# Recurrent gates as three products of rounded and residual parts in place of native fp32, with the first half of the convolution one weight chunk earlier

## What is computed

```python
xc = causal_depthwise_conv(x_lru, conv_w, conv_b)       # 4 taps, 1024 channels
xb = xc.reshape(B, S, 8, 128)                           # 8 blocks of 128 channels
r = sigmoid(einsum('bsgi,gij->bsgj', xb, w_a) + b_a)    # 8 products 128x128 by 128x256
i = sigmoid(einsum('bsgi,gij->bsgj', xb, w_x) + b_x)    # 8 more
log_a = -8 * r * softplus(-lam)
a = exp(log_a)
u = sqrt(-expm1(2 * log_a)) * (i * xc)
h_t = a_t * h_(t-1) + u_t
```

## Time and profile before

| what | value |
|---|---|
| median of 3 runs | 1424.68 us (1423.48 to 1426.31) |
| profiled execution | 1427.16 us |
| its span, first to last instruction | 1425.4 us |
| TensorE busy in the span | 1418.2 us (99%) |
| VectorE, ScalarE busy | 854.3 us (60%), 718.3 us (50%) |
| mean granted TensorE clock | 0.998 of full |

### The profile page before, as it was taken

One profiled execution on the slowest core, in us unless ns is written; L12 is line 12 of the kernel. 1 busy time (PEld: TensorE's weight loads), 2 busy tenths in 40 slices (PEclk: granted clock), 3 DMA queues, 4 the chain that ended last, 5 costly groups with the idle time before them and its releaser, 6 DMA issues. The chain is left out here.

```text
span 1425.4 us, 17665 instructions
## 1 busy us (share of the span) xinstructions
PE 1418.2 (99%) x7194; PEld 1249.3 (88%) x7194; DVE 854.3 (60%) x897; ACT 718.3 (50%) x858; POOL 24.8 (2%) x44
## 2 busy tenths in 40 slices
PE   9999999999999999999999999999999999999999
PEld 7888888888899888998899988998888888888887
DVE  5555545656566655655555655565667787565654
ACT  6644544545545444444344544454664674665642
POOL 2000000000000000000000000000000001000000
PEclk9999999999999999999999999999999999999999
DMA  9455465657556666666666666665555556545574
GB/s 353 157 171 164 152 207 187 194 187 254 192 200 199 205 201 201 203 199 203 205 195 206 205 201 202 203 203 197 195 191 183 171 190 201 183 149 175 184 233 132
DMA packets 78016, 279.16 MB, mean 196 GB/s; under 512 B 8704, under 2 KB 9728, under 8 KB 77552
## 3 DMA queue, kind: packets, MB, share of 16 engines
q1 hardware_dynamic: 76000, 273.06, 57.9%
q0 software_dynamic: 784, 3.08, 0.6%
q10 hardware_dynamic: 1152, 1.90, 0.4%
HBM read 275.91 MB, written 2.10 MB: 195 GB/s over the span
## 5 line engine op out<-in xcount | busy, mean ns | idle before, releaser
L1031 DVE TENSOR_TENSOR w_lo<-raw,w_hi 128x1024 fp32r<-128x1024 f32 x508 | 620.0, 1224 | 520.2 <-ACT w_hi L733 516.3
L733 ACT ACTIVATE w_hi<-raw 128x1024 fp32r<-128x1024 f32 x508 | 534.7, 1056 | 641.2 <-PE banks L420 449.1
L418 PE MATMUL banks<-w_hi,xa 128*128 128x512 f32 x752 | 291.8, 388 | 0.5 <-DVE w_lo L1031 0.5
L418 PE MATMUL banks<-w_hi,xb 128*128 128x512 f32 x768 | 291.8, 380 | 0.0
L419 PE MATMUL banks<-w_lo,xb 128*128 128x512 f32 x768 | 291.1, 379 | 0.0
L420 PE MATMUL banks<-w_hi,xb 128*128 128x512 f32 x768 | 291.1, 379 | 0.0
L420 PE MATMUL banks<-w_hi,xa 128*128 128x512 f32 x752 | 286.0, 380 | 0.0
L419 PE MATMUL banks<-w_lo,xa 128*128 128x512 f32 x752 | 286.0, 380 | 0.0
L442 PE MATMUL banks<-xa,w_hi 128*128 128x512 f32 x1024 | 242.3, 379 | 0.0
L442 PEld LDWEIGHTS banks<-xa,w_hi 128*128 128x128 f32 x1024 | 184.3, 190 | 20.8
L420 PEld LDWEIGHTS banks<-w_hi,xb 128*128 128x128 f32 x768 | 145.2, 189 | 20.6
(11 more groups left out here) (195 smaller groups left out, 605.5 us busy)
## 6 DMA issues: line engine op xcount, KB each, us to landing
raw<-in_weights SPq DMA_DIRECT2D x511, 512.0 KB, 3.9
h<-in_x SPq DMA_DIRECT2D x2, 1024.0 KB, 10.4
arena<-in_x_turned SPq DMA_DIRECT2D x7, 256.0 KB, 6.5
result<-stage ACTq DMA_DIRECT2D x6, 256.0 KB, 4.8
arena<-in_final_norm POOLq DMA_DIRECT2D x1, 1024.0 KB, 7.1
raw<-in_weights SPq DMA_DIRECT2D x2, 256.0 KB, 4.5
arena<-in_gla_b_gate POOLq DMA_DIRECT2D x1, 512.0 KB, 8.3
arena<-in_lru_w_a POOLq DMA_DIRECT2D x1, 512.0 KB, 9.6
```

The source lines that it names most:

```text
L418: pe.matmul(o, xh[:, kt, xs], woven(w_hi, slot, k), start=kt == 0, stop=False)
L733: act.activation(w_hi[:, n % RING, :, :], raw[:, n % RING, :, :], ACT.Copy)\
L1031: dve.tensor_tensor(w_lo[:, n % RING, :, :], raw[:, n % RING, :, :], w_hi[:, n % RING, :, :].bitcast(F32), ALU.subtract).then_inc(lo_ready, 1)
```

## The change

Each native fp32 product of the gates becomes three f32r products. `lru_w` is rounded to `lru_w_hi` by ACT in two instructions (before chunks (20, 3) and (20, 5)), and its residual goes to `lru_w_lo`, over the original, by DVE in two instructions (before (21, 3) and (21, 5)). Each half of `conv` is rounded to `conv_hi` by one ACT instruction before chunk (49, 6) and (51, 6), which waits for `conv_ready`, and its residual goes to `conv_lo` by one DVE instruction before chunk (49, 7) and (51, 7), which waits for `conv_rounded`. Both are stored with even frames first and odd frames behind them, and PE reads them back alternately, in the order of time. PE's wait for `conv_ready` becomes one for `conv_split`, and that for `late_in` one for `lru_w_split`. The taps of half 0 go from chunks 5 and 6 to 4 and 5 of panel 49; those of half 1 stay. `conv_lo` and `conv_hi` lie where `lru_a` and `lru_u` lie, `lru_w_hi` where `cross` lay, and `cross` moves by 2048 elements; five tiles shift by 4 elements. No DMA is added or moved.

```diff
-CONV_TAPS = ({5: (3, 2), 6: (1, 0)}, {5: (3,), 6: (2,), 12: (1,), 13: (0,)})
+CONV_TAPS = ({4: (3, 2), 5: (1, 0)}, {5: (3,), 6: (2,), 12: (1,), 13: (0,)})
...
-        cross = room(2048, 2, 4, S)
+        cross = room(4096, 2, 4, S)
...
+        lru_w_lo = nc.alloc_sbuf_tensor_at("lru_w_lo", [P, 2, 8, P], F32R, offset=arena_at)
+        lru_w_hi = nc.alloc_sbuf_tensor_at("lru_w_hi", [P, 2, 8, P], F32R, offset=arena_at + 4 * 2048)
+        conv_lo = nc.alloc_sbuf_tensor_at("conv_lo", [P, 4, S], F32R, offset=arena_at + 4 * 12304)
+        conv_hi = nc.alloc_sbuf_tensor_at("conv_hi", [P, 4, S], F32R, offset=arena_at + 4 * 13328)
...
+        def in_turns(m):
+            return m.rearrange("p i (a b) -> p i b a", a=2)
+
+        def in_pairs(m):
+            return m.rearrange("p i (b a) -> p i b a", a=2)
...
-                pe.wait_ge(conv_ready, b // 4 + 1)
+                pe.wait_ge(conv_split, b // 4 + 1)
                 if b >= 2:
                     pe.wait_ge(lru_th, b - 1)
                 else:
-                    pe.wait_ge(late_in, 48)
+                    pe.wait_ge(lru_w_split, 2)
                 for i in range(2):
-                    last = pe.matmul(aux[:, b % 2, i * S:(i + 1) * S], lru_w[:, i, b, :],
-                                     conv[:, b % 4, :], start=i == 0, stop=True, skip_group_check=True)
+                    for p, (w, z) in enumerate(((lru_w_hi, conv_hi), (lru_w_hi, conv_lo), (lru_w_lo, conv_hi))):
+                        last = pe.matmul(aux[:, b % 2, i * S:(i + 1) * S], w[:, i, b, :],
+                                         z[:, b % 4, :].rearrange("p (a b) -> p b a", a=2),
+                                         start=i == 0 and p == 0, stop=p == 2, skip_group_check=True)
...
+                if t == FIRST_U + 4 and c in (3, 5):
+                    i = (c - 3) // 2
+                    act.wait_ge(late_in, 48)
+                    act.activation(lru_w_hi[:, i, :, :], lru_w[:, i, :, :], ACT.Copy).then_inc(lru_w_rounded, 1)
+                for j in range(2):
+                    if (t, c) == (FIRST_X + 1 + 2 * j, 6):
+                        act.wait_ge(conv_ready, j + 1)
+                        if j == 1:
+                            act.wait_ge(lru_done, 1)
+                        act.activation(in_turns(conv_hi[:, :, :]), in_pairs(conv), ACT.Copy).then_inc(conv_rounded, 1)
...
+                if t == FIRST_U + 5 and c in (3, 5):
+                    i = (c - 3) // 2
+                    dve.wait_ge(lru_w_rounded, i + 1)
+                    dve.tensor_tensor(lru_w_lo[:, i, :, :], lru_w[:, i, :, :], lru_w_hi[:, i, :, :].bitcast(F32),
+                                      ALU.subtract).then_inc(lru_w_split, 1)
+                for j in range(2):
+                    if (t, c) == (FIRST_X + 1 + 2 * j, 7):
+                        dve.wait_ge(conv_rounded, j + 1)
+                        dve.tensor_tensor(in_turns(conv_lo[:, :, :]), in_pairs(conv),
+                                          in_turns(conv_hi[:, :, :]).bitcast(F32), ALU.subtract).then_inc(conv_split, 1)
```

More of the change, by code:

```diff
@@ L180, in gated_block_kernel @@
         lru_x = room(8192, 4, PAD + S)
[L181 to L185, removed]
+        conv = room(9232, 4, S)
+        th_r = room(10256, 4, S)
+        th_i = room(11280, 4, S)
+        lru_a = room(12304, 4, S)
+        lru_u = room(13328, 4, S)
         y_t = room(8192, 8, S)
@@ L240, in gated_block_kernel @@
         lam_act, lam_ready = sem("lam_act"), sem("lam_ready")
-        conv_ready = sem("conv_ready")
+        conv_ready, conv_rounded, conv_split = sem("conv_ready"), sem("conv_rounded"), sem("conv_split")
+        lru_w_rounded, lru_w_split = sem("lru_w_rounded"), sem("lru_w_split")
         lru_mm, lru_th = sem("lru_mm"), sem("lru_th")
```

## The result

The changed kernel takes 1438.22 us (median of four, 1433.96 to 1439.45) against 1424.68; the ratio is 1.0082 with a 95% interval of 1.0068 to 1.0097. Slower was forecast, and it is slower by 3.6 times the forecast amount: 13.5 us against 3.76, above the stated range of 1426.4 to 1431.4.

The account below looks back on a forecast made before the run. TensorE, 99% busy, was taken to bound the kernel. A gain of 1.52 us against new waits of 1.80 and 3.48 gave +3.76, so 1424.68 becomes 1428.4 us, range 1426.4 to 1431.4.

Parts of the forecast that it names:

- What bounds the kernel, and the gain: TensorE, busy 99%, sets the end; f32r gates cost 1.35 us a pair, gaining 0.38 a pair, 1.52 in all.
- The rounding of the weights: Two ACT and two DVE instructions in panels 20 and 21, 1.06 and 1.22 us each, fit in gaps: cost 0.
- The two waits: TensorE waits at the gates for conv's residual, 1.80 us in the first half, 3.48 in the second; chance 0.68.
- An unpriced cost: Strided writes of conv_hi and conv_lo: plain price taken; above, double, +2.28 us a half, +4.6 in all, chance 0.08.
- The clock falls in the longer wait: Rival: TensorE drops to half speed in the 3.5 us wait at the second gates, +2.6 us, 1431.0; chance 0.08.
- The granted clock is full throughout: Reading of the earlier trace: TensorE's clock is full in all 40 slices, its longest wait in the loop 0.47 us.
- The range: 1426.4 to 1431.4 us: takes in the clock case, leaves out no-wait, dear strided instructions and part of one-wait, about 0.2.
- What is late next: After the gates' waits nothing more is late: splits behind the queued rounding and ACT's tanh come in time.
- ACT has caught up by then: ACT's tanh of blocks 0 and 4 wants results that come later than before, but is not late.

Follow-up runs that it names:

- e7: Changed kernel with conv_hi and conv_lo in plain order, rounding and residual both on VectorE right behind the last tap; 1424.57 us, ratio 0.9991.
- e1: Changed kernel with conv_hi and conv_lo stored in plain order and read by TensorE in plain order; 1431.70 us, ratio 1.0037.
- e10: Changed kernel with conv_lo stored plainly: VectorE's residual reads conv_hi far apart but writes plainly; 1430.41 us, one run.
- e3: Changed kernel with 28 and 44 extra f32r matmuls on TensorE ahead of its two waits for conv_split; 1432.59 us, ratio 1.0044.
- e4: Changed kernel with TensorE's gates multiplying pieces of lru_w_hi and lru_w_lo, ready long before, in place of conv_hi and conv_lo; 1429.42 us, ratio 1.0029.
- e6: Changed kernel with plain storage of conv_hi and conv_lo, and 14 and 28 extra matmuls ahead of TensorE's two waits; 1429.04 us, ratio 1.0027.
- e5: Changed kernel with rounding and residual writing in plain order and reading conv with a step of two elements, same storage; 1433.36 us, ratio 1.0049.
- e9: Changed kernel with plain storage, and ScalarE's rounding of conv one chunk later, behind splits S(49, 6) and S(51, 6); 1428.38 us, ratio 1.0022.
- e8: Changed kernel with the first half's taps back where they were before the change; 1437.52 us, ratio 1.0089.

## Why the prediction was wrong, point by point

- **What bounds the kernel, and the gain**: right. A pair of gates would cost 1.35 at full clock (the second pair ran at 0.11 a matmul), and e7 shows the gain once nothing waits.
- **The rounding of the weights**: right. 1.04 on ScalarE and 1.22 on VectorE, inside the gaps.
- **The two waits**: right in place, order and cause, and in e1 right to 0.03 each. In the changed kernel 3.57 and 5.24 in place of 1.80 and 3.48.
- **"An unpriced cost" is the step that failed first.** I took the plain price for the rounding and the residual because TensorE reads alternately and VectorE reads PSUM with a stride at no loss. Both rows are reads, and the new instructions write. The writes cost 2.06 and 2.05 against 1.06 and 1.22, 1.8 a half. The upper bound of 2.28 a half held, but had 0.08. The Trainium skill, SBUF — State Buffer, in the note on SBUF "cachelines" spoke for it; by that rule far apart reads would cost too, and e10's 1.24 and the earlier trace rows do not bear that out.
- **"The clock falls in the longer wait" is the second**, also with 0.08. I had no row for an idle TensorE of several us and let that count as a reason against. "The granted clock is full throughout" was a wrong reading: the earlier trace rows gives slices of 36 us, in which the fall at 60 us shown above still reads 9, and the mean of 0.998 stood in the table. The rows I took instead, at the start of the span, have a granted clock of 1.00 in the profile's windows (0 to 5 and 5 to 10) and so do not show the low level. The price of 2.6 came near all the same, by luck: each wait cost 2.8 to 2.9. It fell behind both waits of the changed kernel and not only behind the longer one, and cost 5.7, with e3 as the proof. The Trainium skill, TensorE: Matmul & The Clock Gate, on HAM oscillation, has this: long enough idle gaps between bursts bring the half rate; the trace agrees (0.50 at 1105 to 1110).
- **The range** took the rivals one at a time. They were not independent: dearer writes make longer waits, and longer waits let the clock fall. 1.8 + 1.8 + 5.7 on top of 3.8 leaves any range that adds at most one. These three terms are the whole miss in the stretch (12.8 against 3.76, with the old wait 0.25 shorter); the remaining 0.8 of the medians lies within their spread.
- **"What is late next"**: "nothing" was true of this kernel only because the wait covered it. "ACT has caught up by then" was false: e4 shows its tanh 2.8 late at blocks 6 and 7.

The cause is shown, then: e1 takes the writes out, e3 the clock, e6 both, and 3.8 is left, which is the forecast order of waits less the gain; e7 removes these too. What stays open is in which executions the clock falls behind a given wait, and whether it then stays low for 3.4 or 6.8 us: behind 1.5 it held in the profile of e1, behind 2.4 it held in that of e10, behind 2.0 and 2.1 it fell in those of e5 and e9, and behind 2.85 in that of e4.

## What to carry to other kernels

When an engine that is 99% busy gets a new wait, price the wait twice: its length, and the half clock for some us behind it, which here added 5.7 to waits of 8.8. Ask for the granted clock in windows of a few us: the 40 slices of the page hid 6.8 us at half speed in the kernel before. A step that is put where "its input will be ready" holds up all that is queued behind it if the input is late; put it behind the last producer on the same engine, as in e7, and the wait and the queue vanish together. And look for a row of the same kind before pricing a walk over memory: a strided read says nothing of a strided write.

## What the runs showed of the hardware

- Writing 128x1024 f32r elements to SBUF with neighbours 128 elements apart takes 2.05 to 2.07 us on ScalarE and on VectorE, against 1.06 and 1.22 plainly. Reading that way costs VectorE 1.24. Reading with a step of two elements costs ScalarE 1.58 and VectorE 1.22.
- TensorE reads f32r moving operands of 256 columns alternately from two halves at 0.1125 us and in plain order at 0.118: the alternating read is the faster one.
- At the gates TensorE's clock went to half behind every idle gap of 2.85 us or more in these profiles (2.85 in e4 to 5.75 in e8) and behind those of 2.0 (e5) and 2.1 (e9); it held behind 1.5 (e1) and 2.4 (e10). In e5 and e9 it fell only 0.4 and 1.0 us after TensorE had begun again. It also fell behind a gap of 0.78 and 32 matmuls of 7 columns (kernel before). Each low stretch inside the spans lasted 3.4 or 6.8 us, partly under full load.
- Rounding 128x1024 to f32r takes VectorE 0.69 as a copy, less than ScalarE's 1.06.
